# First modulation weights by rows from SP, first unit by GpSimd, rows and constants from ACT; modulated input split by token tiles

## Chip, cores and metric

One core of a Trainium2 chip runs the kernel. The metric is the device time of one execution in microseconds. The profile is of one execution on that core.

## The reference

One layer of a streaming encoder step for 256 prompt tokens and 64 sample tokens, D = 1024, all in float32. The part around the change is its opening:

```
mod = silu(c) @ w_ada + b_ada        # per sequence, w_ada is 1024 x 6144
sh1, sc1, g1, sh2, sc2, g2 = split(mod, 6)
h = rmsnorm(x, norm1_g) * (1 + sc1) + sh1
proj = h @ w_in                      # 1024 x 8192: A q|k|v, B q|k|v, two gates
```

After it come differential attention on A (8 heads, with 256 cached keys), stick-breaking attention on B (16 heads), `x += g1 * (mix @ w_out)`, a second modulated norm with `sh2, sc2`, and a hierarchical mixture of 32 experts, of which each token uses two. The rows of keys and values are outputs too.

## The kernel before

Five engines have a written program each, with semaphores between them. Tokens are padded to 384, three tiles of 128. `x_sb` holds them as rows; `xnT`, `hT_hi` and `hT_lo` hold them as columns (8 blocks k of 128 features by 384 tokens). Each float32 projection is done with three products of parts (`mm3`, L556 to L558): high by high, high by low, low by high. ACT makes a high part by a copy into the rounded type, VectorE the low part by subtracting it. For weights this is `split` (L1051 on ACT, L1339 on VectorE): it takes a unit from `raw[j]` to `w_hi[j]`, `w_lo[j]`. A unit is 384 columns of `w_in`, 128 each of q, k and v of a head, 1.5 MB, loaded by `load_unit` (L357) in three transfers whose pieces are 512 bytes. Unit h uses buffer h % 2, and unit h + 2 is loaded once `split_done` says that unit h has been split.

The opening, before attention, runs like this.

*SP* (L347 to L382) issues constants and small vectors (L347 to L352), two of the eight modulation tiles `ada_buf` (L361), x (L371, L372), nine small loads of which eight are broadcasts to 128 partitions (L374 to L377), waits for GpSimd's fills (`setup_done`), loads the router's weights (L379 to L382), then two more tiles, unit 0, four more tiles (each when its buffer has been used) and unit 1. A tile `ada_buf` is all 1024 rows by 256 columns of `w_ada`, 1 MB in pieces of 1 KB. The first eight tiles are the columns of `sh1` and `sc1`. Behind them SP waits for the transposes of x (`n_T`) and loads the caches and unit 2.

*ACT* and *VectorE* make silu(c) (L1014, L1275 to L1279), TensorE turns it and the vectors to columns (L567), and VectorE pads them (`c_cols`). Then `first_chunks` on TensorE multiplies `c_cols` (128 x 32, of which two columns are used) by four tiles at a time into four groups of 32 partitions of PSUM bank 7, in two turns of 32 matmuls of 256 columns (L561). ACT copies the result to `first_rows` (L1041), after each turn; four transposes (L605) bring it to columns; VectorE adds the bias (`mod_columns`, L1321) and makes `gain1` (L1324).

Meanwhile ACT squares x with a sum (`norm_rows`, L1024), VectorE scales the rows (`scale_rows`, L1299), TensorE transposes them (L580), and ACT and VectorE copy them to `xnT` (L1031, L1304).

The input is then modulated in place: VectorE takes k = 0 to 4 (L1309, two instructions for each k, one for each sequence) and ACT k = 5 to 7 (L1060). ACT makes `hT_hi` in four pieces of two k by 384 tokens (L1064), and VectorE `hT_lo` in the same four pieces (L1353). TensorE's first projection tile (`proj_tile`, L556) waits for each of these pieces (`h_ready`); tiles 1 and 2 need no wait then. From there `a_iteration` runs the heads of A as a pipeline on all engines.

Orders that matter: on ACT, `split(0)` stands between `norm_out` and the second copy to `first_rows`; on VectorE, `split(0, 0)` stands ahead of `mod_columns`. GpSimd has nothing from its fills (L1680 to L1688) until the first head's `rope` (L1696). The first attention buffers share memory with `xn`, and the modulation tiles share it with `hT_hi` and what follows it.

Of the kernel before, what the change touches and what calls it, by code (L numbers as in the profile page):

```python
# [7 lines left out]
P = 128  # L8
D = 1024
KD = D // P  # L10
SEQ, DEC, PAST = 256, 64, 256
TOK = SEQ + DEC
TILES = 3
# [9 lines left out]
EPS = 1e-6  # L23
NEG = -1e30
# [46 lines left out]
DVE_K = 5  # L71
# [8 lines left out]
def build(nc, t_in, t_out):  # L80
    g = t_in
    ctx = ExitStack()
    with ctx:
# [89 lines left out]
        ada_buf = [place(f"ada_buf{n}", [P, KD, ADA_COLS], F32, hT_at + 4 * KD * ADA_COLS * n) for n in range(4)]  # L173
        assert hT_at + 16 * KD * ADA_COLS <= raw_at
        first_rows = place("first_rows", [P, 2, ADA_COLS], F32, hT_at + 16 * KD * ADA_COLS)
        assert hT_at + 16 * KD * ADA_COLS + 8 * ADA_COLS <= raw_at
# [5 lines left out]
        xn = place("xn", [P, TILES, D], F32, attn_at)  # L182

# [90 lines left out]
        c_act = sem("c_act"); c_dve = sem("c_dve"); vecT_done = sem("vecT_done"); vec_ready = sem("vec_ready")  # L274
        raw_loaded = [sem(f"raw_loaded{j}") for j in range(2)]
        ada_in = [sem(f"ada_in{n}") for n in range(4)]; late_in = [sem(f"late_in{n}") for n in range(2)]
        ada_used = sem("ada_used"); late_used = sem("late_used")
        first_out = sem("first_out"); late_out = sem("late_out"); mod_T = sem("mod_T"); mod_ready = sem("mod_ready")
# [3 lines left out]
        h_full = sem("h_full"); h_hi = sem("h_hi"); h_ready = sem("h_ready")  # L282
# [31 lines left out]
        r_log = sem("r_log"); r_sub = sem("r_sub"); r_exp = sem("r_exp"); r_e2 = sem("r_e2"); r_e2x = sem("r_e2x")  # L314
        r_M = sem("r_M"); r_rank = sem("r_rank"); r_count = sem("r_count"); r_rows = sem("r_rows"); r_slot = sem("r_slot"); rounds_ready = sem("rounds_ready")
# [30 lines left out]
        def _(sp):  # L346
            sp.dma_start(cst[:], g["shape_constants"][:, 0:C_ALL]).then_inc(small_in, 16)  # L347
            sp.dma_start(vec_rows[64:72, :], g["c_prompt"].rearrange("a (k p) -> (a k) p", p=P)).then_inc(small_in, 16)
            sp.dma_start(vec_rows[72:80, :], g["c_sample"].rearrange("a (k p) -> (a k) p", p=P)).then_inc(small_in, 16)
            sp.dma_start(vec_rows[0:48, :], g["b_ada"].rearrange("(k p) -> k p", p=P)).then_inc(small_in, 16)  # L350
            sp.dma_start(vec_rows[48:56, :], g["norm1_g"].rearrange("(k p) -> k p", p=P)).then_inc(small_in, 16)
            sp.dma_start(vec_rows[56:64, :], g["norm2_g"].rearrange("(k p) -> k p", p=P)).then_inc(small_in, 16)  # L352

# [6 lines left out]
            def load_ada(c):  # L360
                sp.dma_start(ada_buf[c % 4][:], w_ada3[:, :, c * ADA_COLS:(c + 1) * ADA_COLS]).then_inc(ada_in[c % 4], 16)  # L361
# [6 lines left out]

            load_ada(0)
            load_ada(1)  # L370
            sp.dma_start(x_sb[:, 0:2, :], g["x_prompt"][0].rearrange("(t p) d -> p t d", p=P)).then_inc(x_in, 16)  # L371
            sp.dma_start(x_sb[0:DEC, 2, :], g["x_sample"][0]).then_inc(x_in, 16)  # L372
            for n, name in enumerate(("a_lam_q1", "a_lam_k1", "a_lam_q2", "a_lam_k2")):
                sp.dma_start(lam_rows[:, n, :], g[name].partition_broadcast(P)).then_inc(rows_in, 16)  # L374
            for n in range(4):
                sp.dma_start(gqk[:, n, :], g["a_qnorm_g" if n < 2 else "a_knorm_g"].partition_broadcast(P)).then_inc(rows_in, 16)
            sp.dma_start(subln[:], g["a_subln_g"].rearrange("(p a) -> p a", a=1)).then_inc(rows_in, 16)  # L377
# [1476 lines left out]
```

## Time and profile before

| | us |
|---|---|
| Median of three runs | 897.12 (896.08 to 897.85) |
| The profiled execution | 899.36 |
| Its span | 897.6 |
| TensorE busy | 739.8 (82%), 5329 matmuls |
| VectorE busy | 379.0 (42%) |
| ACT busy | 256.0 (29%) |
| GpSimd busy | 98.9 (11%) |
| Moved by transfers | 199.17 MB, mean 222 GB/s |

In the profile, PE is TensorE's matmuls and PEld its weight loads, DVE is VectorE, ACT is ScalarE, POOL is GpSimd and SP the engine that only issues transfers; SPq and POOLq are the issuing of transfers and of register work. L followed by a number is a line of the kernel. A row of the timeline gives start, duration, the instruction with output and inputs, shapes as partitions x elements, how many were merged, and in brackets how long the engine had been idle and what released it. The busy time of matmuls contains their overlap. The granted clock is a share of TensorE's full clock; its two levels are 1.2 and 2.4 GHz.

### The profile page before, as it was taken

The page shows a single profiled execution, that of the slowest core. Times are in us where ns is not written, and L with a number is a line of the kernel's source. Part 1 is how long each engine was busy: PE and PEld are TensorE (multiplying, and loading weights), DVE is VectorE, ACT ScalarE, POOL GpSimd, SP SyncE. Part 2 cuts the span into 40 slices and gives each one's busy share as a digit, 9 for nine tenths or more (in the row PEclk, how much of TensorE's full clock was granted, in tenths as well). Part 3 has the DMA queues.
Part 4 walks back from the last instruction along what each step waited for, and adds up shares of the span by engine and source line. Part 5 has one row for each costly group of instructions (what it writes and reads, how often), then busy time and mean ns, then how long its engine had stood idle before and what let it go on. Part 6 is the DMA issues. An engine that isn't in the chain of part 4 may idle for free.

```text
span 897.6 us, 13728 instructions
## 1 busy us (share of the span) xinstructions
PE 739.8 (82%) x5329; PEld 611.2 (68%) x5329; DVE 379.0 (42%) x554; ACT 256.0 (29%) x453; POOL 98.9 (11%) x156
## 2 busy tenths in 40 slices
PE   2679899999769989999998996955899878888770
PEld 1359888888659979998987996933555455464440
DVE  2243555555547553443334675561332322313223
ACT  2243444444432324543452232220111111101100
POOL 0001111111100000011100000011011010110014
PEclk9679999999999999999998998965999999999985
DMA  7955355555453649434223444089899999999805
GB/s 222 332 158 153 98 177 178 183 169 172 150 187 107 192 117 289 131 96 111 73 74 108 141 140 141 2 348 416 359 392 418 418 418 417 418 418 418 342 19 175
DMA packets 141032, 199.17 MB, mean 222 GB/s; under 512 B 11688, under 2 KB 124728, under 8 KB 128696
## 3 DMA queue, kind: packets, MB, share of 16 engines
q1 hardware_dynamic: 135208, 189.07, 60.1%
q0 software_dynamic: 5776, 9.45, 3.2%
q8 instruction: 32, 0.52, 0.2%
q14 instruction: 16, 0.13, 0.0%
HBM read 193.47 MB, written 16.55 MB: 234 GB/s over the span
## 4 chain that ended last, share of the span: by engine, by line
PE 55%; issue 23%; DVE 6%; ACT 6%; DVEq 5%; POOLq 2%; POOL 2%; ACTq 1%; DMA 0%
PE ps L561 31%; PE ps L556 6%; PE ps L557 6%; PE ps L558 6%; DVEq L1439 2%; ACT w_hi L1051 2%; DVEq L1435 1%; ACT probs L1124 1%; PE ps L936 1%; PE ps L940 1%; PE ps L972 1%; PE ps L714 1%; DVEq L1506 1%; PE ps L685 1%; DVE ss L1374 0%
## 5 line engine op out<-in xcount | busy, mean ns | idle before, releaser
L561 PE MATMUL ps<-e_w,xgT 128*64 128x256 f32 x1024 | 130.0, 418 | 32.2 <-issue 30.9
L561 PEld LDWEIGHTS ps<-e_w,xgT 128*64 128x64 f32 x1024 | 91.0, 151 | 66.9 <-issue 38.7
L1339 DVE TENSOR_TENSOR w_lo<-raw,w_hi 128x2048 fp32r<-128x2048 f32 (+1 forms) x36 | 100.1, 2780 | 35.2 <-ACT w_hi L1051 35.2
L556 PE MATMUL ps<-hT_hi,w_hi 128*128 128x320 f32 x320 | 102.2, 319 | 7.5 <-DVE w_lo L1339 7.3
L558 PE MATMUL ps<-hT_hi,w_lo 128*128 128x320 f32 x320 | 99.5, 311 | 0.0
L557 PE MATMUL ps<-hT_lo,w_hi 128*128 128x320 f32 x320 | 99.5, 311 | 0.0
L1051 ACT ACTIVATE w_hi<-raw 128x2048 fp32r<-128x2048 f32 (+1 forms) x36 | 83.4, 2316 | 54.8 <-PE ps L558 54.6
L1628 DVE TENSOR_SCALAR h_s<-h_e 128x256 f32<-128x256 f32 x16 | 4.7, 295 | 162.7 <-ACT h_e L1244 162.7
L556 PE MATMUL ps<-w_hi,hT_hi 128*128 128x384 f32 x192 | 68.2, 355 | 5.2 <-DVE hT_lo L1353 5.2
L556 PEld LDWEIGHTS ps<-hT_hi,w_hi 128*128 128x128 f32 x320 | 60.8, 190 | 9.9 <-DVE w_lo L1339 6.5
L558 PE MATMUL ps<-w_hi,hT_lo 128*128 128x384 f32 x192 | 66.1, 344 | 0.0
L557 PE MATMUL ps<-w_lo,hT_hi 128*128 128x384 f32 x192 | 66.1, 344 | 0.0
L557 PEld LDWEIGHTS ps<-hT_lo,w_hi 128*128 128x128 f32 x320 | 60.8, 190 | 0.0
L558 PEld LDWEIGHTS ps<-hT_hi,w_lo 128*128 128x128 f32 x320 | 60.7, 190 | 0.0
L561 PE MATMUL ps<-e_w,hidT 128*64 128x512 f32 x256 | 58.4, 598 | 0.6 <-ACT hidT L1250 0.6
L1244 ACT ACTIVATE h_e<-ps 128x256 f32<-128x256 f32 x16 | 6.1, 384 | 153.7 <-PE ps L561 153.7
L556 PEld LDWEIGHTS ps<-w_hi,hT_hi 128*128 128x128 f32 x192 | 37.4, 195 | 10.0 <-issue 10.0
L556 PE MATMUL ps<-oT_hi,w_hi 128*128 128x320 f32 x128 | 40.4, 316 | 1.1 <-DVE oT_lo L1465 1.1
L557 PE MATMUL ps<-oT_lo,w_hi 128*128 128x320 f32 x128 | 40.2, 314 | 0.0
L558 PE MATMUL ps<-oT_hi,w_lo 128*128 128x320 f32 x128 | 40.0, 313 | 0.0
L1793 POOL DMA_INDIRECT expert_rows<-y_sb,idx x16 | 16.3, 1017 | 215.4 <-DVE y_sb L1641 215.4
L561 PE MATMUL ps<-ada_buf,c_cols 128*32 128x256 f32 x128 | 22.8, 533 | 18.8 <-DMA ada_buf<-in_w_ada 18.8
(251 smaller groups left out, 1249.0 us busy)
## 6 DMA issues: line engine op xcount, KB each, us to landing
e_w<-in_w SPq DMA_DIRECT2D x96, 1024.0 KB, 19.6
raw<-in_w_in SPq DMA_DIRECT2D x48, 512.0 KB
ada_late<-in_w_ada SPq DMA_DIRECT2D x16, 1024.0 KB, 5.3
ada_buf<-in_w_ada SPq DMA_DIRECT2D x8, 1024.0 KB, 7.8
raw<-in_w_in SPq DMA_DIRECT2D x8, 1024.0 KB
raw<-in_w_oa SPq DMA_DIRECT2D x4, 1024.0 KB
raw<-in_w_ob SPq DMA_DIRECT2D x4, 1024.0 KB
raw<-in_w_out SPq DMA_DIRECT2D x4, 1024.0 KB
```

Source lines behind the costliest of these rows:

```text
L556: nc.tensor.matmul(out, lhs_hi, rhs_hi, start=first, stop=False, skip_group_check=True)
L557: nc.tensor.matmul(out, lhs_hi, rhs_lo, start=False, stop=False, skip_group_check=True)
L558: return nc.tensor.matmul(out, lhs_lo, rhs_hi, start=False, stop=last, skip_group_check=True)
L561: return nc.tensor.matmul(out, lhs, rhs, start=first, stop=last, skip_group_check=True)
L685: last = nc.tensor.transpose(ps[:, 4, t * P:(t + 1) * P], o_n[:, t, :], ident)
L714: last = nc.tensor.transpose(ps[:, b, c * P:(c + 1) * P], amap[:, n * P:(n + 1) * P], ident)
L936: last = nc.tensor.transpose(ps[:, 0, k * P:(k + 1) * P], xg[p % RING][:, k:D:KD], ident)
L940: last = nc.tensor.transpose(ps[:, 1, (k - 4) * P:(k - 3) * P], xg[p % RING][:, k:D:KD], ident)
L1051: A(w_hi[j][:, :, 0:width], raw[j][:, :, 0:width], ACT.Copy).then_inc(split_hi, 1)
L1339: V.tensor_tensor(w_lo[j][:, :, 0:width], raw[j][:, :, 0:width], f32(w_hi[j][:, :, 0:width]), ALU.subtract).then_inc(split_done, 1)
L1439: dve.drain()
L1793: G.indirect_dma_start(y_dram, bass.IndirectOffsetOnAxis(ap=idx[:, 1, p:p + 1], axis=0), y_sb[j][:], None, bounds_check=2 * TOK, oob_is_er ...
```

## The change

- `ada_buf` is gone. SP issues the two vectors c and then eight row blocks `ada_first[k]`: 128 rows of `w_ada` by the 2048 columns of `sh1` and `sc1`, 1 MB each in pieces of 8 KB. Three of them lie at the end of memory. TensorE's `first_columns` uses one block at a time: for each k four matmuls of 512 columns, one into each group of 32 partitions of bank 7. It waits for k = 0, 1, 2 together, for 3, 4, 5 together, for 6 and for 7. The first three k come ahead of the transposes of x, the others behind them.
- SP then issues unit 1, waits for the fills, and loads the router's weights. Before the caches it also waits for the last use of the row blocks (`ada_used`).
- ACT issues x, the constants, `b_ada` and the norm vectors at its start, and the nine small loads behind the exponential of c and ahead of the norm.
- GpSimd issues unit 0 behind its fills, with a semaphore of its own.
- ACT copies the modulation rows once (512 columns), behind `split(0)`. `lam_exp` and the sums for lambda stand behind `norm_out`.
- The modulated input goes to a buffer of its own, `h_full`, all of it by VectorE, tile by tile of tokens and in halves of four k. ACT makes `hT_hi` and VectorE `hT_lo` in the same six halves, with the multiply-adds of the next tile between the low parts. Each of the three first projection tiles waits for its two halves.
- Several semaphores are put together (`vecT_done` and `mod_T` to `col_T`; those of the router to `r_log`, `r_arg`, `r_exp`) with counts in place of names.

```diff
+ADA_GROUP = (0, 0, 0, 1, 1, 1, 2, 3)
-DVE_K = 5
...
+        ada_at = [hT_at + 8 * D * k for k in range(5)] + [(end - 24 * D) // 32 * 32 + 8 * D * k for k in range(3)]
+        ada_first = [place(f"ada_first{k}", [P, 2 * D], F32, ada_at[k]) for k in range(KD)]
+        h_full = place("h_full", [P, KD, PADDED], F32, attn_at + 4 * (2 * TILES * UNIT + 8 * P))
...
         def _(sp):
-            sp.dma_start(cst[:], g["shape_constants"][:, 0:C_ALL]).then_inc(small_in, 16)
...
+            def load_first(k):
+                sp.dma_start(ada_first[k][:], w_ada3[:, k, 0:2 * D]).then_inc(ada_in[ADA_GROUP[k]], 16)
...
-            load_ada(0)
-            load_ada(1)
...
+            for k in range(KD):
+                load_first(k)
+            load_unit(0, 1, 1)
             sp.wait_ge(setup_done, 1)
...
-            load_ada(2)
-            load_ada(3)
-            load_unit(0, 0, 0)
-            for c in range(4, 8):
-                sp.wait_ge(ada_used, c - 3)
-                load_ada(c)
-            load_unit(0, 1, 1)
...
             sp.wait_ge(n_T, KD)
+            sp.wait_ge(ada_used, KD)
...
+            def first_columns(ks):
+                for k in ks:
+                    pe.wait_ge(ada_in[ADA_GROUP[k]], 16 * ADA_GROUP.count(ADA_GROUP[k]))
+                    for j in range(4):
+                        last = mm(ps[32 * j:32 * j + 32, 7, :], c_cols[:, k, :], ada_first[k][:, j * 512:(j + 1) * 512],
+                                  k == 0, k == KD - 1)
+                    last.then_inc(ada_used, 1)
+
+            first_columns(range(3))
             pe.wait_ge(n_scaled, 3)
             for k in range(KD - 1):
                 rows_to_columns(xn, k, k).then_inc(n_T, 1)
             pe.wait_ge(n_out_a, 1)
             rows_to_columns(xn, KD - 1, 0).then_inc(n_T, 1)
-            pe.wait_ge(first_out, 1)
-            first_chunks(1)
-            pe.wait_ge(first_out, 2)
+            first_columns(range(3, KD))
+            pe.wait_ge(n_out_a, 5)
             pe.wait_ge(n_out_v, 3)
...
-                    if first and t == 0 and k % 2 == 0:
-                        pe.wait_ge(h_ready, k // 2 + 1)
+                    if first and k % 4 == 0:
+                        pe.wait_ge(h_ready, 2 * t + k // 4 + 1)
...
             A = nc.scalar.activation
+            act.dma_start(x_sb[:, 0:2, :], g["x_prompt"][0].rearrange("(t p) d -> p t d", p=P)).then_inc(x_in, 16)
+            act.dma_start(x_sb[0:DEC, 2, :], g["x_sample"][0]).then_inc(x_in, 16)
+            act.dma_start(cst[:], g["shape_constants"][:, 0:C_ALL]).then_inc(small_in, 16)
...
             act.wait_ge(small_in, 96)
             A(c_sig[64:80, :], vec_rows[64:80, :], ACT.Exp, scale=-1.0).then_inc(c_act, 1)
...
+            for n, name in enumerate(("a_lam_q1", "a_lam_k1", "a_lam_q2", "a_lam_k2")):
+                act.dma_start(lam_rows[:, n, :], g[name].partition_broadcast(P)).then_inc(rows_in, 16)
...
             act.wait_ge(x_in, 32)
             norm_rows(xn)
+            norm_out()
             act.wait_ge(lam_dve, 1)
...
+            split(0, None, None)
+            act.wait_ge(ada_used, KD)
+            A(first_rows[:], ps[:, 7, :], ACT.Copy).then_inc(n_out_a, 1)
...
+            for t in range(TILES):
+                for half in range(2):
+                    ks = slice(4 * half, 4 * half + 4)
+                    act.wait_ge(h_mod, 2 * t + half + 1)
+                    A(hT_hi[:, ks, t * P:(t + 1) * P], h_full[:, ks, t * P:(t + 1) * P], ACT.Copy).then_inc(h_hi, 1)
...
+            first_full(0, 0)
+            first_full(0, 1)
+            for t in range(TILES):
+                first_low(t, 0)
+                if t < 2:
+                    first_full(t + 1, 0)
+                first_low(t, 1)
+                if t < 2:
+                    first_full(t + 1, 1)
...
+            for n in range(3):
+                pool.dma_start(raw[0][:, :, n * P:(n + 1) * P], w_in3[:, :, n * D:n * D + P]).then_inc(unit0_in, 16)
```

`first_full(t, half)` is four multiply-adds of 128 columns into `h_full`, `first_low(t, half)` one subtraction of 512 columns behind ACT's high part of that half.

## Rows read from the trace of the kernel before

**Rows 1.** The page: the span in 40 equal slices, TensorE's busy tenths.
```profile
PE   2679899999769989999998996955899878888770
```

**Rows 2.** The list of waits, 0 to 70 us: total, times, longest.
```profile
PE ps L561 <- DMA ada_buf<-in_w_ada: 18.8, 4, 9.8
```

**Rows 3.** Windows; columns: us, engines busy (count), granted clock, DMA share, GB/s.
```profile
2.00:4.00 2.00, 0.00 (x0) 0.00 (x0) 0.00 (x0) 0.10 (x1) 0.91 (x2) 1.00 0.47 138
...
8.00:10.00 2.00, 0.00 (x0) 0.00 (x0) 0.00 (x0) 0.00 (x0) 0.00 (x0) 1.00 1.09 353
...
12.00:12.50 0.50, 0.50 (x6) 0.27 (x4) 0.00 (x0) 0.00 (x0) 0.00 (x0) 1.00 1.07 426
...
14.00:16.00 2.00, 2.00 (x14) 1.09 (x12) 0.00 (x0) 0.57 (x1) 0.00 (x0) 1.00 0.67 112
...
46.00:48.00 2.00, 2.00 (x14) 1.18 (x12) 0.00 (x0) 0.00 (x0) 0.00 (x0) 0.57 1.15 289
...
56.00:58.00 2.00, 0.62 (x2) 0.65 (x3) 1.72 (x2) 2.00 (x4) 0.00 (x0) 0.63 0.16 43
...
600.00:610.00 10.00, 5.53 (x22) 4.99 (x22) 6.58 (x32) 0.20 (x1) 0.98 (x2) 0.50 1.01 427
```

**Rows 4.** The timeline, 0 to 70 us; columns: start us, us, engine, line, operation, [idle before].
```profile
11.45 5.66 PE L561 MATMUL ps<-ada_buf,c_cols 128*32 128x256 f32 x32 [4.68 <-DMA ada_buf<-in_w_ada]
...
15.43 1.06 ACT L1024 ACTIVATE xn<-x_sb 128x1024 f32<-128x1024 f32 x1 [10.74 <-DMA x_sb<-in_x_sample]
...
19.39 2.07 DVE L1299 TENSOR_SCALAR xn<-x_sb,rstd 128x1024 f32<-128x1024 f32 x3
...
33.31 2.84 PE L580 MATMUL ps<-cst,xn 128*128 128x128 f32 x24
...
36.24 2.76 ACT L1051 ACTIVATE w_hi<-raw 128x3072 fp32r<-128x3072 f32 x1
...
39.03 3.36 DVE L1339 TENSOR_TENSOR w_lo<-raw,w_hi 128x3072 fp32r<-128x3072 f32 x1 [2.29 <-ACT w_hi L1051]
...
45.70 5.33 PE L561 MATMUL ps<-ada_buf,c_cols 128*32 128x256 f32 x32 [2.02 <-DMA ada_buf<-in_w_ada]
...
51.08 0.38 ACT L1041 ACTIVATE first_rows<-ps 128x256 f32<-128x256 f32 x1 [12.07 <-PE ps L561]
...
51.51 0.66 PE L605 MATMUL ps<-cst,first_rows 128*128 128x128 f32 x4 [0.47 <-ACT first_rows L1041]
...
52.20 0.26 DVE L1321 TENSOR_TENSOR mod<-ps,vec_cols 128x16 f32<-128x16 f32 x2 [9.81 <-PE ps L605]
...
52.89 2.83 DVE L1309 TENSOR_SCALAR xnT<-xnT,gain,mod 128x256 f32<-128x256 f32 x10 [0.17 <-issue]
...
55.40 3.05 ACT L1064 ACTIVATE hT_hi<-xnT 128x768 fp32r<-128x768 f32 x4
...
56.28 3.56 DVE L1353 TENSOR_TENSOR hT_lo<-xnT,hT_hi 128x768 fp32r<-128x768 f32 x4 [0.56 <-ACT hT_hi L1064]
...
57.38 0.66 PE L556 MATMUL ps<-w_hi,hT_hi 128*128 128x384 f32 x1 [5.21 <-DVE hT_lo L1353]
...
63.28 0.37 PE L556 MATMUL ps<-w_hi,hT_hi 128*128 128x384 f32 x1
```

**Rows 5.** The same timeline, SP's issues.
```profile
4.14 1.22 SPq L371 DMA_DIRECT2D x_sb<-in_x_prompt  x1
...
6.04 0.58 SPq L374 DMA_DIRECT2D lam_rows<-in_a_lam_q  x1
...
10.62 0.72 SPq L377 DMA_DIRECT2D subln<-in_a_subln_g  x1
```

**Rows 6.** The transfers, issues by line: count, KB each, median us to landing.
```profile
h_rows<-h2tok POOLq DMA_DIRECT2D x3, 512.0 KB, 8.5
```

**Rows 7.** The timeline, GpSimd's issues of plain transfers near the end.
```profile
873.89 0.60 POOL L1817 DMA_DIRECT2D ya<-expert_rows  x1 [2.20 <-DMA expert_rows<-y_sb,idx]
...
876.09 0.56 POOL L1817 DMA_DIRECT2D ya<-expert_rows  x1
```

More of the change, by code:

```diff
@@ L737, in _ @@
                 last = nc.tensor.transpose(ps[:, 5 + n // 4, (n % 4) * P:(n % 4 + 1) * P], late_rows[:, n * P:(n + 1) * P], ident)
-            last.then_inc(mod_T, 1)
+            last.then_inc(col_T, 1)
             pe.wait_ge(a_olo, 8)
@@ L906, in _ @@
             mm(ps[:, 0, EXPERTS:3 * EXPERTS], ones[:], flat[:, 0:2 * EXPERTS], False)
-            mm(ps[:, 0, 2 * EXPERTS:3 * EXPERTS], ones[:], M[:, 0, :], False).then_inc(r_rank, 1)
+            mm(ps[:, 0, 2 * EXPERTS:3 * EXPERTS], ones[:], M[:, 0, :], False).then_inc(r_log, 1)
             for t in range(TILES):
                 last = mm(ps[:, 1, 0:EXPERTS], ones[:], M[:, t, :], t == 0, t == 2)
-            last.then_inc(r_count, 1)
+            last.then_inc(r_log, 1)
             def slot_table(r):
@@ L1329, in _ @@
             scale_rows(xn, 1)
+            norm_out()
+            dve.wait_ge(rows_in, 144)
+            for n in range(2):
+                V.tensor_tensor(lam_prod[:, n, :], lam_rows[:, 2 * n, :], lam_rows[:, 2 * n + 1, :], ALU.mult)
+            V.tensor_scalar(gqk[:, 0:2, :], gqk[:, 0:2, :], 0.125, None, ALU.mult)
+            V.tensor_scalar(subln[:], subln[:], 1.0 - LAM_INIT, None, ALU.mult)
+            dve.drain()
+            V.tensor_reduce(lam_sum[:], lam_prod[:], AX, ALU.add).then_inc(lam_dve, 1)
             dve.wait_ge(lam_act, 1)
@@ L1342, in _ @@
             split(0, 0)
[L1343 to L1344 removed]
+            dve.wait_ge(col_T, 2)
+            mod_columns(0, [ps[:, 5, :].rearrange("p (m j s) -> p j m s", m=4, j=4)[:, :, :, 0:2]],
                         gain1, 8, 48)
@@ L1347, in _, with first_full, first_low @@
             dve.wait_ge(n_out_v, 4)
-            for k in range(DVE_K):
-                modulate(xnT, xnT[:, k, :], k, gain1, 0).then_inc(h_full, 1)
-            for n in range(4):
-                ks = slice(2 * n, 2 * n + 2)
-                dve.wait_ge(h_hi, n + 1)
-                V.tensor_tensor(hT_lo[:, ks, :], xnT[:, ks, :], f32(hT_hi[:, ks, :]), ALU.subtract).then_inc(h_ready, 1)
+            def first_full(t, half):
+                for k in range(4 * half, 4 * half + 4):
+                    last = V.tensor_scalar(h_full[:, k, t * P:(t + 1) * P], xnT[:, k, t * P:(t + 1) * P], gain1[:, k, t // 2:t // 2 + 1],
+                                           mod[:, k, t // 2:t // 2 + 1], ALU.mult, ALU.add)
+                last.then_inc(h_mod, 1)
+            def first_low(t, half):
+                ks, sl = slice(4 * half, 4 * half + 4), slice(t * P, (t + 1) * P)
+                dve.wait_ge(h_hi, 2 * t + half + 1)
+                V.tensor_tensor(hT_lo[:, ks, sl], h_full[:, ks, sl], f32(hT_hi[:, ks, sl]), ALU.subtract).then_inc(h_ready, 1)
+            first_full(0, 0)
[7 more added lines that the diff above has]
+                    first_full(t + 1, 1)
             def combine(parts, f):
@@ L1568, in _ @@
             tt(eh2[:], etie[:], bc(etm[:], 8), ALU.is_equal)
-            V.tensor_tensor(e2[:], m2[:], m1[:], ALU.subtract).then_inc(r_e2, 1)
+            V.tensor_tensor(e2[:], m2[:], m1[:], ALU.subtract).then_inc(r_arg, 1)
             for n, eh in enumerate((eh1, eh2)):
```

104 lines of the change are left out of this document (32 added, 72 removed).

## The prediction

> **What bounds the kernel now.** I read the page first. In its forty slices TensorE is at seven tenths or more nearly everywhere, except for two holes: the first two slices (0 to 45 us) and two slices at 583 to 628 us, the router and the first experts [rows 1]. The change works in the first hole. There the list of waits for 0 to 70 us says what TensorE lacks: 18.8 us in four waits for tiles of the modulation weights, by far its longest [rows 2]. The windows say why. The transfers run at their limit, but the rate depends on what is moved: 353 GB/s with the 1 KB pieces of the modulation tiles, 426 with the 4 KB rows of x, 289 with the 512 B pieces of a projection unit, and 427 near 600 us with expert weights; at 14 to 16 us it falls to 112 GB/s behind small transfers [rows 3]. So the opening is bound by transfers and by what stands ahead of what in SP's queue. Last I read the timeline from the last modulation matmul (starts at 45.70, ends at 51.03) to the first projection matmul at 57.38; from there TensorE works without a hole of note, with the granted clock at 0.5, and returns to its full level at 63.28 [rows 4]. Whatever makes 57.38 earlier should move the whole rest: nothing behind it waits for a time of its own, only for earlier work.
>
> The profiled execution took 899.36 us with a span of 897.6; the median is 897.12. I work out a shift of the span and subtract it from the median. Some 0.2% (1.8 us) can be told from no change.
>
> **Part 1, transfers ahead of the last modulation row.** Before, the eight 1 MB column tiles share SP's queue with x, nine small loads (eight of them broadcasts), four router loads and unit 0's three. After, SP issues two tiny loads and then eight row blocks (one k each, 8 KB pieces); x, constants and broadcasts go by ACT, unit 0 by GpSimd, and unit 1 and the router stand behind. Large pieces ahead of the end are 8.39 MB of weights, 1.31 of x and 0.25 of constants, 9.95 MB. Bounds are 28.2 us at 353 GB/s and 23.4 at 426; 8 KB pieces are nearest to the 4 KB rows of x, so I take 415 GB/s: 24.0 us. Unit 0 is 1.57 MB; if it shares the engines in that time it adds 5.4 us at 289 GB/s, if it comes wholly behind, nothing; I take 5.4. The broadcasts add at most the 1.3 us of the row at 14 to 16 us (0.67 of two microseconds) and at least nothing; I take 1.3 with a little for the b_ada and norm rows, 1.5. The stream starts within the window from 2 to 4 us, where 138 GB/s ran [rows 3]: 2.5. From the last byte to the semaphore I allow 1.5 (no row has it alone; ends 0 and 2). Sum: the last row block lands at 2.5 + 24.0 + 5.4 + 1.5 + 1.5 = 34.9 us. Call it T.
>
> The Trainium skill (DMA: Bandwidth & Descriptors, Specifications) puts the limit of HBM per core at about 358 GB/s. By that the large pieces would take 27.8 us and the gain would be 3.8 us smaller. The rows at 426 and 427 GB/s do not agree with it, so the sum does not use it.
>
> **Part 2, from T to the first projection matmul.** Thirty-two matmuls of 256 columns took 5.66 us at 11.45, or 0.177 each; of 512 columns 0.354. The fourth group's four matmuls take 1.4 us. Earlier row blocks arrive every 3 us and need 1.4 each, so TensorE has kept up by T: k 3 to 5 wait for one another, but the 16 matmuls of k 3 to 6 are 5.7 us and the two blocks behind them take about 6 to arrive. Then, by the timeline [rows 4]: ACT copies 512 columns in one piece (0.38 us for 256, so 0.6), four transposes 0.66 and 0.1 between them: T + 2.8. Modulation columns and gain took from 52.20 to ahead of 52.89, about 0.6 with their drains, the same here: T + 3.4. Before, VectorE then did ten multiply-adds in 2.83 us (ACT six beside it), ACT the high parts in 3.05 us for four of 768 columns, VectorE the low parts in 3.56. After, four multiply-adds of 128 columns (0.28 mean before for longer ones, so 0.2 each) end at T + 4.2, ACT's first high part (512 columns, 0.55) at T + 4.8, VectorE's second four at T + 5.0, its first low part (0.6) at T + 5.7, and TensorE starts at T + 5.8 = 40.7. The old stretch from the last matmul was 57.38 - 51.03 = 6.35 us, the new one 4.4: splitting by token tiles is worth 2.0, the queues the rest. Gain: 57.38 - 40.7 = **16.7 us**.
>
> All multiply-adds now go to VectorE, 24 of 0.2 us and six low parts of 0.6, so 1.4 us per half of a tile. TensorE needs 3.8 us for that half at the slow clock (12 matmuls, 0.32 apart) and 2.1 at the full one. The six halves hide behind it; if that cover were gone they would cost 5 to 6 us.
>
> **Part 3, the clock.** Before, TensorE paused 5.2 us ahead of the projection, the clock fell in the window 56 to 58 (0.63 there, 0.50 after), and 57.38 to 63.28 ran at the 1.2 GHz level: at 2.4 GHz that is 2.95 us less. Now the pause is 3.0 us. It may keep the clock (gain 2.95) or not (0). I take **1.5**.
>
> **Part 4, what is moved and must stay hidden.** *ACT* issues x, its sample, constants and three small loads: x took SP 1.22 us and a small one 0.58, so some 4.1 us for the six [rows 5], while nothing is there to compute. Then nine small issues stand between the sigmoid's exponential and the norm; on SP they went from 6.04 to 11.34, 5.3 us. Behind them the norm takes 4.0 (from 15.43 to the scaling at 19.39), scaling 2.1, 24 transposes 2.8 [rows 4]. If constants land at 10.5 (1.6 MB at half of 400 GB/s from 2.5 on), the norm starts at 16, scaling ends at 22 and transposes at 25; cost 0 behind the weights that arrive until 34.9. *Unit 0*: ACT's split of 2.76 us stands ahead of the copy of modulation rows, and VectorE's of 3.36 ahead of the modulation columns [rows 4]. They cost 0 if unit 0 has landed 6.2 us ahead of T + 2.8, by 31.5 us. Its waits queue both engines' whole rest, so each later microsecond costs one. A transfer issued by GpSimd beside a busy queue is shown by the stores of 512 KB: 8.5 us to landing [rows 6], 62 GB/s; by that, unit 0 lands at 3.2 (GpSimd's last two fills lie in the window 2 to 4) + 25.4 + 2 = 30.6, just in time, and with an even share near 15. Bounds 0 and the price in the rival below; I take 0. *SP* now waits for the last use of the row blocks before the caches and unit 2: 36.3 plus unit 1's 5.4 us, while ACT needs unit 1 at about 46 and unit 2 at about 59 (17 us ahead of the old times): 0. The router is wanted near 590. The semaphores put together late in the kernel keep their order: 0.
>
> **Sum:** 16.7 + 1.5 = 18.2 us; 897.1 - 18.2 = 878.9, forecast **879.0**.
>
> **Rivals.** *Unit 0 comes late.* For it: the three loads are 3072 pieces of 512 B against 64 large ones per transfer engine, and the 62 GB/s above. If its share is half of that (31 GB/s), 0.85 MB is there when the weights end at about 31, the other 0.72 MB goes beside unit 1 at 145 GB/s, and it lands at 37.5. Then 6.2 for the splits and 2.9 for modulation and the first half: TensorE starts at 46.6, the gain is 10.8, the time 886.3. Against it: its issue starts as early as the weights'. The Trainium skill (DMA: Bandwidth & Descriptors, Queues, rings and completion order) has each transfer engine go round its queues a packet at a time; if SP's packets are the larger ones, that would give GpSimd such a small share. No row of this trace shows packets of that kind.
>
> *Constants or x come late.* They have one queue, constants behind x, and the sigmoid waits for all. From their landing s the ACT path needs 0.3 + 5.3 + 4.0 + 2.1 + 2.8 = 14.5, then 20 matmuls of 7.1 us: s + 21.6 against T + 1.4 = 36.3. So from s = 14.7 each microsecond costs one. Three even shares give 1.6 MB at 137 GB/s, s = 14.2, on the edge. At s = 20 the cost is 5.3 and the time 884.2. For it: x took until 15.43 before; against: it was issued 4 us later then and stood behind 2 MB.
>
> *Slower: GpSimd makes the pieces too slowly.* GpSimd took 0.60 us for an issue with 128 pieces and 0.56 for one with 64 [rows 7]. If all of 0.60 were per piece (4.7 ns), unit 0 would need 14.4 us; the two rows speak for far less. Break-even is a landing at 57.4 - 9.1 = 48.3, which is 14 ns a piece; at 20 ns it lands at 66, TensorE starts at 75.5, and the time is 915.
>
> *It does nothing*: the transfers' total sets the end whatever their order. For it speaks that the engines were saturated; against, that 1.57 MB of unit 1 and the router are now behind, and the wasted windows gone.
>
> **Chances.** Forecast (876 to 882) 0.52; unit 0 late 0.20; constants late 0.20; nothing 0.03; slower 0.05. Range: fast end with 426 GB/s, no broadcasts and the full clock, 18.2 + 0.6 + 1.5 + 1.4 = 21.7, and 3 more if unit 0 takes less of the engines: 872.5. Slow end: both late cases, 888.5. Faster 0.92, same 0.03, slower 0.05.
>
> **What would show it.** First projection matmul near 41 (right between 37 and 44); last row block's matmuls from about 35; ACT's first split before 31.5; the stretch between them 4.4 us; ACT's norm at about 16; a rate near 415 GB/s until 30 us. TensorE waiting for low parts inside the first unit would refute part 2; an unchanged distance from that first matmul to the end is the premise, and if it grows by over 2 us the premise is wrong.

## The result: 8.2 us faster, where 18.1 were forecast

The changed kernel took 888.42 us (median of 4 runs, 888.03 to 889.46), the kernel before in the same session 896.60 (4 runs, 896.04 to 897.85): ratio 0.9907, 95% interval 0.9892 to 0.9921. The sign was right. The time lies on the upper edge of the range (872.5 to 888.5), 9.4 us from the forecast of 879.0, and the gain is less than half of the forecast one. The profiled execution took 888.03 us with a span of 886.3; before it was 899.36 and 897.6.

TensorE's slices on the page of the changed kernel answer to [rows 1]:

```profile
PE   0589999998789889999998978864899788798770
```

The first slice (22 us) holds next to no matmul, the second half, and the third is at eight tenths. The hole at 600 us is as it was. The waits of the opening (engine, what it waited for: us in total, times, longest), against [rows 2]:

```profile
ACT c_sig L1000 <- DMA vec_rows<-in_norm_g: 11.5, 1, 11.5
ACT lam_exp L1029 <- DVE lam_sum L1315: 7.1, 1, 7.1
DVE lam_prod L1311 <- DMA subln<-in_a_subln_g: 5.7, 1, 5.7
PE ps L585 <- ACT first_rows L1043: 4.8, 1, 4.8
PE ps L545 <- DMA ada_first<-in_w_ada: 2.5, 2, 1.3
```

TensorE's wait for modulation weights fell from 18.8 us to 2.5. In its place stands a wait that no part of the prediction has: VectorE's first lambda operation waits 5.7 us for the last of the nine small loads, ACT's lambda exponential waits 7.1 us for VectorE, and TensorE waits 4.8 us for ACT's copy of the modulation rows. The kernel before had the first of these waits too, where it held nothing up: unit 0 was split only at 36.24 [rows 4].

```profile
18.55 0.36 DVE L1290 TENSOR_TENSOR lam_prod<-lam_rows 128x64 f32<-128x64 f32 x2 [10.98 <-DMA subln<-in_a_subln_g]
```

The timeline of the opening (start, duration, engine, line, operation, tiles, count, idle time before and its releaser), to be laid beside [rows 4]:

```profile
16.95 0.30 ACT L1000 ACTIVATE c_sig<-vec_rows 16x128 f32<-16x128 f32 x1 [11.48 <-DMA vec_rows<-in_norm_g]
...
20.66 5.24 PE L545 MATMUL ps<-ada_first,c_cols 128*32 128x512 f32 x24 [1.33 <-DMA ada_first<-in_w_ada]
20.72 0.45 ACTq L1023 DMA_DIRECT2D subln<-in_a_subln_g  x1
21.28 1.06 ACT L1010 ACTIVATE xn<-x_sb 128x1024 f32<-128x1024 f32 x1 [4.02 <-issue]
...
27.31 2.84 PE L564 MATMUL ps<-cst,xn 128*128 128x128 f32 x24 [1.41 <-DVE xn L1277]
...
34.92 1.07 PE L545 MATMUL ps<-ada_first,c_cols 128*32 128x512 f32 x8 [1.20 <-DMA ada_first<-in_w_ada]
...
36.46 0.36 DVE L1311 TENSOR_TENSOR lam_prod<-lam_rows 128x64 f32<-128x64 f32 x2 [5.72 <-DMA subln<-in_a_subln_g]
...
37.42 0.20 ACT L1029 ACTIVATE lam_exp<-lam_sum 128x2 f32<-128x2 f32 x1 [7.06 <-DVE lam_sum L1315]
37.53 2.75 ACT L1039 ACTIVATE w_hi<-raw 128x3072 fp32r<-128x3072 f32 x1
...
40.18 0.58 ACT L1043 ACTIVATE first_rows<-ps 128x512 f32<-128x512 f32 x1
40.30 3.36 DVE L1324 TENSOR_TENSOR w_lo<-raw,w_hi 128x3072 fp32r<-128x3072 f32 x1 [2.26 <-ACT w_hi L1039]
...
43.58 0.18 DVE L1299 TENSOR_TENSOR mod<-ps,vec_cols 128x32 f32<-128x32 f32 x1
...
44.19 2.14 DVE L1337 TENSOR_SCALAR h_full<-xnT,gain,mod 128x128 f32<-128x128 f32 x8 [0.17 <-issue]
...
47.08 0.66 PE L540 MATMUL ps<-w_hi,hT_hi 128*128 128x384 f32 x1 [5.15 <-DVE hT_lo L1345]
```

Read it from the middle. The last row block has landed at 34.92, where T was forecast as 34.9, and its matmuls end at 35.99. From there the forecast goes 4.4 us to the first projection matmul; the trace takes 11.1. ACT stood idle from 30.35 until 37.42. In its program the order is: copies of the transposed x, lambda exponential, split of unit 0, copy of the modulation rows. In VectorE's it is: lambda block, low part of unit 0, modulation columns. Both programs put the first wait for the nine small loads ahead of unit 0's split, so the 2.75 and 3.36 us that should have been hidden ran after the weights had landed. From 43.58 on the order is that of the forecast again, in 3.50 us where the forecast has 3.0.

The transfers (how each was issued, count, KB of one, median us to landing), the packets on GpSimd's queue from 0 to 45 us (count, MB, share), and two-microsecond stretches of the windows (busy time of the engines, granted clock, DMA share, GB/s):

```profile
raw<-in_w_in POOLq DMA_DIRECT2D x3, 512.0 KB, 14.4
...
lam_rows<-in_a_lam_q ACTq DMA_DIRECT2D x2, 32.0 KB, 10.1
...
gqk<-in_a_qnorm_g ACTq DMA_DIRECT2D x2, 32.0 KB, 15.9
```

```profile
q0 software_dynamic: 432, 1.57, 9.2%
```

```profile
14.00:16.00 2.00, 0.00 (x0) 0.00 (x0) 0.00 (x0) 0.00 (x0) 0.00 (x0) 1.00 1.05 368
...
22.00:24.00 2.00, 2.00 (x12) 0.45 (x8) 0.00 (x0) 2.00 (x5) 0.00 (x0) 1.00 1.04 403
...
50.00:52.00 2.00, 2.00 (x7) 2.00 (x7) 2.00 (x8) 0.88 (x2) 0.00 (x0) 0.50 0.47 117
```

The stretch at 14 us with 112 GB/s [rows 3] is gone. The eight broadcasts of 32 KB, issued by ACT beside SP's row blocks, took 7.9 to 16.0 us to land (the rows give medians of two). Unit 0, the load that the prediction feared for, was issued in three transfers from 3.73 on, and the last of them landed at 23.6, long before ACT could split it. The prediction counted 3072 pieces of 512 bytes for it; on GpSimd's queue stand 432 packets for its 1.57 MB.

### The profile page after: what moved, and what is told of

It is laid out like the page before. It is cut to its first block, busy times and chain, and to the rows that moved or that the text cites. A ratio compares the mean times of both kernels' runs of the same rounds, so it can differ in the third digit from the quotient of the medians.

```text
span 886.3 us, 13607 instructions
## 1 busy us (share of the span) xinstructions
PE 727.3 (82%) x5265; PEld 601.5 (68%) x5265; DVE 382.6 (43%) x569; ACT 254.1 (29%) x448; POOL 101.2 (11%) x159
## 4 chain that ended last, share of the span: by engine, by line
PE 54%; issue 22%; ACT 6%; DVE 5%; DVEq 5%; POOL 2%; POOLq 2%; DMA 2%; SPq 1%; ACTq 1%
PE ps L545 31%; PE ps L540 6%; PE ps L542 6%; PE ps L541 6%; DVEq L1441 2%; ACT w_hi L1039 2%; DVEq L1437 1%; PE ps L916 1%; SPq L353 1%; ACT probs L1110 1%; PE ps L920 1%; DMA raw<-in_w_in 1%; PE ps L952 1%; DVEq L1508 1%; DMA out_a_v_sample<-stage 1%
## 5 line engine op out<-in xcount | busy, mean ns | idle before, releaser
L540 PEld LDWEIGHTS ps<-w_hi,hT_hi 128*128 128x128 f32 x192 | 37.0, 193 | 10.1 <-issue 10.1
L545 PEld LDWEIGHTS ps<-e_w,hidT 128*64 128x64 f32 x256 | 17.5, 136 | 29.6 <-issue 27.8
```

Source lines behind the costliest of these rows:

```text
L540: nc.tensor.matmul(out, lhs_hi, rhs_hi, start=first, stop=False, skip_group_check=True)
L545: return nc.tensor.matmul(out, lhs, rhs, start=first, stop=last, skip_group_check=True)
```

## The experiments

**Theory A:** the lambda wait, that is the landing of the nine small loads on a queue beside large pieces, holds unit 0's split, and costs some 7 us. **Rival B:** the late constants (16.95 instead of 10.5) are the cause, since they delay everything on ACT. **Rival C:** unit 0 by GpSimd takes the engines' time, or the token split brings nothing.

**Lambda late (e1).** The lambda block goes behind the six halves on VectorE, and its exponential behind the high parts on ACT; nothing else changes.

```diff
 # shortened; ACT
-            act.wait_ge(lam_dve, 1)
-            A(lam_exp[:], lam_sum[:], ACT.Exp).then_inc(lam_act, 1)
 def split ... split(0) ... first_rows ... high parts
+            act.wait_ge(lam_dve, 1)
+            A(lam_exp[:], lam_sum[:], ACT.Exp).then_inc(lam_act, 1)
 # DVE: the block from wait_ge(rows_in, 144) to neg_lam likewise,
 # from ahead of split(0, 0) to behind the loop of first_low and first_full
```

> The changed kernel took 888.4 us, with the first projection matmul at 47.08, although the last weight row block landed as forecast (its matmuls end at 35.99). Here the wait for the nine small loads, the sums for lambda and the exponential move behind the six halves of the modulated input on VectorE and ACT. Theory A (the lambda wait, met at 36.46 by the landing of the last small load, holds ACT's split of unit 0 from about 30.5 to 37.53): ACT's split starts at 30 to 31, the first projection matmul at 41 to 42, time 882 to 883. Rival B (constants landing at 16.9 delay the ACT path and with it everything): nothing moves, 888. Rival C (unit 0 from GpSimd lands only at about 36 to 37): the split still starts at 36 to 37, 887 to 888.

It took 881.11 us (879.3 to 881.14, 5 runs); ratio 0.9841 [0.982, 0.986], against 895.66 of the kernel before. Its timeline:

```profile
16.24 0.30 ACT L1000 ACTIVATE c_sig<-vec_rows 16x128 f32<-16x128 f32 x1 [10.92 <-DMA vec_rows<-in_norm_g]
...
29.54 2.76 ACT L1037 ACTIVATE w_hi<-raw 128x3072 fp32r<-128x3072 f32 x1
...
34.03 1.06 PE L545 MATMUL ps<-ada_first,c_cols 128*32 128x512 f32 x8 [1.02 <-DMA ada_first<-in_w_ada]
...
36.51 0.19 DVE L1300 TENSOR_TENSOR mod<-ps,vec_cols 128x32 f32<-128x32 f32 x1 [0.83 <-PE ps L585]
...
40.01 0.66 PE L540 MATMUL ps<-w_hi,hT_hi 128*128 128x384 f32 x1 [3.54 <-DVE hT_lo L1335]
```

The split runs at 29.54, under the weights, and the first projection matmul starts 7.1 us earlier than in the changed kernel. Of that, 0.9 us is not the wait: the last row block's matmuls start at 34.03 instead of 34.92. From the end of these matmuls to the first projection matmul it is 4.92 us instead of 11.09, so the wait is worth 6.2. The constants were as late as there (16.24), and it cost nothing: the split still ended ahead of the last row block. That shows A and takes away B as a cause. The interval lies clear of that of the changed kernel (0.9892 to 0.9921).

**Constants ahead of x (e2).** ACT issues constants and norm rows first, then x.

```diff
+            act.dma_start(cst ...); act.dma_start(vec_rows ...)   # three of them
             act.dma_start(x_sb[:, 0:2, :], ...)
             act.dma_start(x_sb[0:DEC, 2, :], ...)
-            act.dma_start(cst ...); act.dma_start(vec_rows ...)   # three of them
```

> ACT issues the constants, b_ada and the norm vectors ahead of x, nothing else is changed. Theory A: constants land by 7, the exponential of c and with it the nine small issues come about 10 us sooner (from 7 instead of 17), the last of them lands before 31, so the lambda wait is met in time: first projection matmul at 41 to 42, 882 to 883. Rival B expects the same time, but with the gain from the c path. Rival C: 888. If the small loads are starved by SP's large pieces until these end near 35, whenever they are issued, the wait is met at 35 to 36 and the time stays at 887 to 888.

888.85 us (888.18 to 894.38, 7 runs), ratio 0.994 [0.9919, 0.9962]: no better than the changed kernel.

```profile
7.51 0.30 ACT L1000 ACTIVATE c_sig<-vec_rows 16x128 f32<-16x128 f32 x1 [2.27 <-DMA vec_rows<-in_norm_g]
...
10.40 5.47 ACTq L1022 DMA_DIRECT2D gqk<-in_a_knorm_g  x2
15.90 5.27 ACTq L1023 DMA_DIRECT2D subln<-in_a_subln_g  x1
...
24.53 1.06 ACT L1010 ACTIVATE xn<-x_sb 128x1024 f32<-128x1024 f32 x1 [16.71 <-DMA x_sb<-in_x_sample]
...
39.17 0.36 DVE L1311 TENSOR_TENSOR lam_prod<-lam_rows 128x64 f32<-128x64 f32 x2 [3.73 <-DMA subln<-in_a_subln_g]
```

The constants landed 9.4 us earlier, and the first small load was issued 9.4 us earlier; yet lambda started 2.7 us later. x, issued at 2.65 instead of 0.82 and so behind the first row block's issue, came only at 24.5, and the small loads stood behind it on ACT's queue: the first of them landed at 28.1. ACT's last two kinds of issue took 5.47 and 5.27 us, where they take 0.94 and 0.45 in the changed kernel, so the issue of the last one, for which lambda waits, ended at 21.17 in both. This run therefore tells little of an earlier issue. It shows that constants ahead of x bring nothing; theory A's 882 did not come, and the time lies near the 887 to 888 that stood for small loads starved by large pieces.

**Token split alone (e3).** The kernel before with only the split by token tiles (its queues as they were).

```diff
 # shortened
-            for k in range(DVE_K): modulate(...)      # whole rows of 384 tokens, ACT the rest
+            first_full(0, 0); first_full(0, 1); for t in range(TILES): first_low ... first_full
-                    if first and t == 0 and k % 2 == 0: pe.wait_ge(h_ready, k // 2 + 1)
+                    if first and k % 4 == 0: pe.wait_ge(h_ready, 2 * t + k // 4 + 1)
```

> The kernel before with one part of the change alone: modulated input in a buffer of its own, by VectorE, in six halves of token tiles. The changed kernel shows 3.5 us from the modulation columns to the first projection matmul, before it was 5.2. Theory (part 2 of the prediction): worth 1.7 to 2.0 us, 894.7 against 896.6. Rival: VectorE's larger share makes TensorE wait inside the first unit, or the clock falls sooner, and nothing is gained, 896.6.

893.53 us (889.9 to 899.81, 12 runs), ratio 0.9983 [0.9967, 1.0]. The stretch from the modulation columns to the first projection matmul:

```profile
52.68 0.26 DVE L1319 TENSOR_TENSOR mod<-ps,vec_cols 128x16 f32<-128x16 f32 x2 [10.07 <-PE ps L606]
...
56.25 0.48 PE L557 MATMUL ps<-w_hi,hT_hi 128*128 128x384 f32 x1 [3.61 <-DVE hT_lo L1357]
```

It is 3.57 us, where before it was 5.18 (52.20 to 57.38, [rows 4]): 1.6 us, and the median agrees with about that, though its interval just reaches 1.

**The other way round (e7).** e1 with the modulation of the kernel before, and TensorE's waits for its four pieces.

```diff
 # shortened
-            first_full(0, 0); first_full(0, 1); for t in range(TILES): first_low ... first_full
+            for k in range(DVE_K): modulate(...)      # whole rows of 384 tokens, ACT the rest
```

> The version with the lambda part late, with the modulated input as in the kernel before (in place, five k on VectorE, three on ACT, pieces of two k by 384 tokens). On the kernel before, the token tiles gave 2.1 us (893.5 against 895.7, interval ending at no change). Theory: without them the first projection matmul is 1.7 us later, 882.8 against 881.1, and the change of the queues alone, once its wait is out of the way, is worth the other 13. Rival: the six halves bring nothing here, 881.1.

884.3 us (881.87 to 889.59, 5 runs), ratio 0.9858 [0.9832, 0.9884].

```profile
37.51 0.19 DVE L1305 TENSOR_TENSOR mod<-ps,vec_cols 128x32 f32<-128x32 f32 x1 [1.28 <-PE ps L587]
...
42.62 0.66 PE L542 MATMUL ps<-w_hi,hT_hi 128*128 128x384 f32 x1 [5.15 <-DVE hT_lo L1334]
```

From the columns to the projection 5.11 us against 3.50 in e1: 1.6 us again. The last row block's matmuls start 1.0 us later than in e1 (35.03), with the same transfers. The two medians differ by 3.2 us, on two chips, and their intervals overlap, so the split's worth is read from the stretch.

**Unit 0 by SP behind the row blocks (e4).**

```diff
-            for n in range(3): pool.dma_start(raw[0] ...)   # ahead, on GpSimd
+            for n in range(3): sp.dma_start(raw[0] ...)     # on SP, ahead of unit 1
```

> The changed kernel with unit 0 issued by SP, behind the eight row blocks and ahead of unit 1, in place of GpSimd. Theory A: the last row block lands 4 to 5 us sooner (about 31), unit 0 only some 6 us behind it, near 37, so the split starts at about 37 by another wait, and the first projection matmul stays near 46 to 47: 887 to 889. Rival C (GpSimd's transfer was the late one): sooner by 2 us or more, under 886.5.

886.24 us (883.98 to 891.0, 6 runs), ratio 0.9899 [0.988, 0.9919].

```profile
36.33 2.76 ACT L1041 ACTIVATE w_hi<-raw 128x3072 fp32r<-128x3072 f32 x1 [3.26 <-DMA raw<-in_w_in]
...
45.89 0.66 PE L542 MATMUL ps<-w_hi,hT_hi 128*128 128x384 f32 x1 [5.15 <-DVE hT_lo L1347]
```

Without unit 0 beside them the last row block landed at 28.9 instead of 34.9; the prediction's price for sharing was 5.4 us. TensorE used it up at 31.2 without waiting for it, held by the transposes. But then unit 0 itself is the last to land and the split starts at 36.33, 1.2 us earlier than in the changed kernel. GpSimd's loads cost T about what was priced and are not the cause. The median lies just under the 886.5 that stood for rival C, but its interval overlaps that of the changed kernel, and the trace has unit 0 later than there, not sooner.

**The nine small loads by SP ahead of the row blocks (e5).**

```diff
+            for n, name in enumerate(("a_lam_q1", ...)): sp.dma_start(lam_rows ...)   # and gqk, subln
             for k in range(KD): load_first(k)
-            for n, name in enumerate(("a_lam_q1", ...)): act.dma_start(lam_rows ...)  # and gqk, subln
```

> The changed kernel, lambda wait in its place, but the nine small loads issued by SP ahead of the row blocks, not by ACT behind the exponential of c. With the constants first on ACT they had been issued from 7.5 and still landed only at 39.2. Theory (on ACT's queue they land only when SP's large pieces end; on SP's queue, ahead of them, they do not wait): the last lands before 20, the lambda wait costs nothing, the split of unit 0 starts at 26 to 30, and the first projection matmul is at 41 to 44, since the row blocks are issued some 5 us later while x and unit 0 use the engines: 881.5 to 885. Rival (it is the place of the wait alone and small loads are slow on any queue): 888.

886.48 us (885.16 to 892.42, 6 runs), ratio 0.9901 [0.9872, 0.993].

```profile
6.00:8.00 2.00, 0.00 (x0) 0.00 (x0) 0.00 (x0) 0.00 (x0) 0.59 (x1) 1.00 0.66 174
8.00:10.00 2.00, 0.00 (x0) 0.00 (x0) 0.00 (x0) 0.00 (x0) 0.00 (x0) 1.00 0.61 188
...
38.00:40.00 2.00, 1.98 (x20) 0.68 (x24) 1.42 (x8) 0.79 (x2) 0.00 (x0) 1.00 0.27 99
```

```profile
38.27 0.35 DVE L1311 TENSOR_TENSOR lam_prod<-lam_rows 128x64 f32<-128x64 f32 x2
...
49.05 0.66 PE L545 MATMUL ps<-w_hi,hT_hi 128*128 128x384 f32 x1 [3.54 <-DVE hT_lo L1345]
```

Lambda no longer waits for a transfer, as A says. But the last row block's matmuls start at 43.06 instead of 34.92, and the first projection matmul comes 2.0 us later. The trace shows three things on the way. SP issues its first row block at 7.61 instead of 1.64, behind the nine. The rate from 6 to 10 us is 174 and 188 GB/s, where the changed kernel has 253 and 379. And the last row block comes in apart: a transfer lands in sixteen parts, and of this one twelve had landed by 37.1 and the last at 43.0 (34.1 to 34.9 in the changed kernel), while the engines were busy for 0.27 of the time from 38 to 40 us. What held these few engines is open. The wait went, and its price came back through the transfers.

**Row blocks in pieces of 2 KB (e8).** If small pieces wait their turn behind 8 KB pieces of another queue, shorter pieces there must bring the small loads in sooner, with the same bytes and the same issuing engines.

```diff
-                sp.dma_start(ada_first[k][:], w_ada3[:, k, 0:2 * D]) ...
+                for q in range(4):
+                    sp.dma_start(ada_first[k][:, q * 512:(q + 1) * 512], ...)
...
-                    pe.wait_ge(ada_in[ADA_GROUP[k]], 16 * ADA_GROUP.count(ADA_GROUP[k]))
+                    pe.wait_ge(ada_in[ADA_GROUP[k]], 64 * ADA_GROUP.count(ADA_GROUP[k]))
```

> The changed kernel with each row block loaded by four transfers of 512 columns, so SP's pieces are 2 KB, not 8 KB; order, bytes and the lambda wait stay. Theory (the pieces of ACT's queue take turns with SP's, so a small load pays for a large piece each time: the eight broadcasts are 64 pieces for each of 16 transfer engines and took from about 17 to 35.5, 0.29 us each, and an 8 KB piece at 410 GB/s over 16 engines takes 0.32): with 2 KB pieces the constants land by 12 instead of 17 and the last small load by 26 instead of 36.4, the split of unit 0 starts when the norm's copies are out, at 24 to 28, and the first projection matmul is at 40 to 43, 881 to 884. Rival (small loads are slow whatever stands beside them, or ACT's queue is served last): the lambda wait ends at 34 to 37 again, 887 to 889.

887.06 us (884.0 to 890.37, 6 runs), ratio 0.9897 [0.9874, 0.9919]. Its issues and its timeline:

```profile
lam_rows<-in_a_lam_q ACTq DMA_DIRECT2D x2, 32.0 KB, 7.7
...
gqk<-in_a_qnorm_g ACTq DMA_DIRECT2D x2, 32.0 KB, 9.2
```

```profile
11.17 0.31 ACT L1001 ACTIVATE c_sig<-vec_rows 16x128 f32<-16x128 f32 x1 [5.77 <-DMA vec_rows<-in_norm_g]
...
33.03 0.35 DVE L1312 TENSOR_TENSOR lam_prod<-lam_rows 128x64 f32<-128x64 f32 x2
...
39.88 1.07 PE L546 MATMUL ps<-ada_first,c_cols 128*32 128x512 f32 x8 [1.66 <-DMA ada_first<-in_w_ada]
```

The broadcasts landed in 7.7 to 10.0 us instead of 10.1 to 15.9 (medians of two), the constants let the sigmoid start at 11.17 instead of 16.95, and lambda waited for no transfer. The last small load landed at 27.3 instead of 36.4; 5.8 us of that is its earlier issue, 3.3 its faster landing. The spacing tells more. In the changed kernel the first four broadcasts landed 2.6 us apart (24.9, 27.5, 30.2, 32.8), and 0.3 to 0.4 us apart once the last row block had landed at 34.9; with 2 KB pieces all eight landed 0.8 to 1.1 us apart. So the size of the pieces beside them sets their pace. The gain is given back: the rate at 10 to 16 us is 312 to 324 GB/s where the 8 KB pieces had 347 to 371, and the last row block comes 5.0 us later. The median is that of the rival (887 to 889), and the forecast of 881 to 884 failed by the row blocks. The Trainium skill (DMA: Bandwidth & Descriptors, Queues, rings and completion order) says that a transfer engine serves its queues in turn, a packet at a time; e8 agrees in kind, and no run here shows how large a packet is.

**A warm clock (e6, e10).** e1 and four matmuls of 512 columns between the transposes and the projection, into a bank that is free.

```diff
             last.then_inc(col_T, 1)
+            for _ in range(4):
+                mm(ps[:, 6, :], ident, first_rows[:, 0:512], True)
```

> The version with the lambda part late (881.1 us, first projection matmul at 40.01), with four matmuls of 128x128 by 512 columns on finished data into an idle bank, between the transposes of the modulation rows and the first projection tile (their result is not used). Part 3 of the prediction: TensorE's pause of 3.5 us there let the granted clock fall to 0.5 until 45.5, with matmuls 0.32 us apart for 0.175. If the pause is the cause, the clock stays at its full level, that stretch is 2.5 to 2.9 us shorter, and the time is 878.3 to 878.8. Rival: the level depends on the thinner work ahead of the pause (waits for row blocks), the clock falls anyway, 881, or 882 if the four get in the way.

e6 took 880.02 us (878.27 to 885.83, 5 runs), ratio 0.9816 [0.9793, 0.9839]. Against e1's 0.9841 that decided nothing, so both were run again, on one chip with the changed kernel.

> The changed kernel once more, unchanged, on the same chip as the three below, so that they can be compared with it: 888.4 us, first projection matmul at 47.

> The version with the lambda part late, unchanged, beside the changed kernel on one chip: 7 us less than it (881.3 against 888.4), as the places of the first projection matmul say (40.0 against 47.1).

> The version with the lambda part late and four filling matmuls, unchanged, beside the version without them. With the filling, the clock stayed at its full level from the transposes on, and the first tile's matmuls ran 0.175 us apart. Theory: 1.5 to 2.7 us less than the version without (878.6 to 880). Rival (the 1.1 us between the two medians came from the chips): the same time.

The kernel before took 896.58 us there (11 runs), and e8 above belongs to the same series. The changed kernel: 885.87 (884.15 to 890.52, 6 runs), 0.9889 [0.9865, 0.9913]. e9, which is e1: 880.55 (879.61 to 884.06, 5 runs), 0.9837 [0.9812, 0.9863]. e10, which is e6: 880.33 (879.24 to 880.92, 5 runs), 0.9825 [0.9804, 0.9846]. The changed kernel showed the same wait again:

```profile
37.00 0.36 DVE L1311 TENSOR_TENSOR lam_prod<-lam_rows 128x64 f32<-128x64 f32 x2 [6.24 <-DMA subln<-in_a_subln_g]
```

The window from 42 to 44 us and GpSimd's multiplication by the norm gains (minimum, median and maximum ns; first and last start) in e9:

```profile
42.00:44.00 2.00, 2.00 (x8) 2.00 (x7) 2.00 (x7) 0.94 (x2) 0.00 (x0) 0.50 0.73 213
```

```profile
L1700 POOL TENSOR_TENSOR stage<-stage,gqk x8: 1839/1850/1853, 60.2 to 215.2; 128x768 f32<-128x768 f32 x8
```

and in e10:

```profile
42.00:44.00 2.00, 2.00 (x13) 2.00 (x13) 2.00 (x8) 0.70 (x2) 0.00 (x0) 1.00 0.63 176
```

```profile
L1702 POOL TENSOR_TENSOR stage<-stage,gqk x8: 1844/1849/1860, 57.4 to 212.3; 128x768 f32<-128x768 f32 x8
```

(There the last row block's matmuls end at 36.69 and the first projection matmul starts at 47.61; in e9 these are 35.43 and 40.76.) The filler kept the clock at its full level, and the work that follows the first unit came 2.8 us earlier and stayed so until 215 us; 0.2 of that is the start of the projection (40.52 against 40.76). At the first matmul of the output projection nothing of it was left (250.60 in e9, 250.38 in e10). The stretch between took 35.4 us in e9 and 38.1 in e10, but also 35.0 and 38.0 in two executions of the kernel before (its trace and b1 below), so a single pair of traces can't tell whether the filler lengthened it. The medians are the same, where 1.5 to 2.7 us had been expected.

**The kernel before again (b1)**, one execution, for what differs from one to the next.

> The kernel before once more, for a second profile. Its first profile took 899.36 us, 2 to 4 us more than its timed runs. If the excess lies in the opening, the first projection matmul is near 57.4 again with a long time, or at 54 to 55 with a short one, and the distance from there to the end stays at 839 to 840. If it lies behind the opening, that distance varies by some 3 us.

898.9 us, span 897.2, first projection matmul at 58.01, and from it to the end 839.2 us (840.2 in the trace of the kernel before). It is again 2.9 us above its median (896.04). Over all fourteen traces the rest behind the first projection matmul takes 838.1 to 839.3 us in the four whose execution was within 0.6 us of its kernel's median (the changed kernel, e1, e9, e10), and 839.2 to 845.3 in the other ten, whose executions were 2.8 to 6.3 us above. So at least a part of such an excess lies behind the opening.

## Why the prediction was half right

- *What bounds the kernel:* right. The stretch from the first projection matmul to the end was 840.2 us before and 839.2 after (839.3 in e1): what the opening gives, the rest keeps. It is no constant, though: 841.2 in the changed kernel's second trace, 843.4 in e4, 845.3 in e7.
- *Part 1, transfers:* right, T = 34.9 forecast and 34.92 measured. It is partly luck: the rate was 347 to 379 GB/s from 8 to 16 us and 400 to 415 from 22 on, where 415 was taken throughout, and other terms made up for it. Its 5.4 us for unit 0 is borne out by e4, where the last row block landed 6.0 us earlier.
- *Part 2, from T to the projection:* 40.7 forecast, and e1 has it at 40.01 (e9 at 40.76). From the end of the last row block's matmuls it takes 4.92 us (5.33 in e9) where I had 4.4: mostly, the multiply-adds took 0.27 us each, not 0.2. The token split is worth 1.6 us, not 2.0. TensorE did not wait for a low part inside the first unit. In the changed kernel the step does not hold: see part 4.
- *Part 3, the clock:* 1.5 taken, 0 came. The granted clock is 0.50 in the window from 50 to 52 us. The stretch's own worth of 2.95 us is about right (2.5 in e10), but it does not reach the median.
- *Part 4, what must stay hidden:* **here the prediction failed.** The step says of the nine small loads that their issues take 5.3 us and leaves it at that; it follows ACT's chain through the norm and the transposes to 25 us and gives "cost 0 behind the weights that arrive until 34.9". It never asked when these loads land and who waits for them. The last landed at 36.4, and the wait stands ahead of unit 0's split on both engines. Measured from the end of the last row block's matmuls it cost 11.09 - 4.92 = 6.2 us (5.6 by a1 and e9); the medians say 5.3 on one chip (885.87 - 880.55) and 7.3 across two sessions. That is nearly all of the 6.4 us by which the first projection matmul missed its forecast (47.08 against 40.7). The trace before could have warned: there VectorE waited 11.0 us for the same small load, until 18.55.
- *The constants* were late, 16.95 against 10.5, and by the rival's own rule each microsecond from 14.7 on should have cost one: 2.3 us. It cost nothing (e1). By the rule the last row block's matmuls end 21.6 us behind the constants, at 38.6. In the trace the way through the transposes took 13.2 us and not 14.5, and the 20 matmuls behind them, which I had priced at 7.1 us from a row of matmuls with half the columns [rows 4], took 3.64 and 1.07 (a matmul of 512 columns stands there as two records, hence x32 and x8). That is 34.9, and TensorE still waited 1.2 us for the last row block.
- *The rivals:* unit 0 late (886.3) gives nearly the measured time, but unit 0 was there at 23.6. The right number would have had the wrong cause: what the case shares with it is only the place, the split ahead of the modulation rows. GpSimd's pieces came at no great price, and "does nothing" and "slower" fell.
- *The sum:* 18.2 less 6.2 for the wait and 1.5 for the clock is 10.5. The first projection matmul came 10.3 us earlier, the profiled pair says 11.3 and the medians 8.2. The kernel before has a profiled execution 2.8 us above its median (899.36 to 896.60), and the changed kernel's first has not (888.03 to 888.42), though its second has (890.52 to 885.87 in a1). So a shift read from a profiled pair is not the shift of the medians. The 2 us between 10.5 and 8.2 stay unexplained.

The best version is e1: 0.984 of the time of the kernel before, and against the changed kernel on one chip 5.3 us less, for moving one block of eight small operations. e10 is equal to it.

## What to carry to other kernels

When transfers are moved to other queues, price for each the time at which it lands and find the first instruction that waits for it, also for the smallest: a 32 KB load may need 16 us beside 8 KB pieces. In an engine's program put a wait for something that is needed late behind the work that is needed now; here that order alone was worth 5 to 7 us. Three attempts to bring the load in earlier were worth nothing: in two (e5, e8) the large transfers came later by nearly as much or more (5.0 and 8.1 us), and in the third (e2) the load itself came no earlier. Forecast from medians if there are some, and keep the profiled execution for shifts within a stretch.

## What the runs showed of the hardware

- The landing of small transfers depends on the piece size of another queue. Each of the eight broadcasts is 128 pieces of 256 B, 8 for each of 16 transfer engines. Beside 8 KB pieces they landed 2.6 us apart, 0.33 us a small piece; at 410 GB/s one of 16 engines needs 0.32 us for 8 KB. Beside 2 KB pieces (e8) they landed some 0.9 us apart, 0.11 us a small piece; at 315 GB/s 2 KB need 0.10. That is an estimate, and it fits one small piece for each large one. The first of them took 7.9 us to land, and 7.2 in e8, so this part does not go by the piece size.
- Issuing can itself stall: with x still on its way on ACT's queue, its issues of `gqk` and `subln` took 5.47 and 5.27 us (e2) against 0.94 and 0.45. In the changed kernel SP's three issues of unit 1, behind eight row blocks, took from 6.45 to 35.2.
- The parts of one transfer can land far apart: with the nine small loads ahead of the row blocks (e5), the last row block's sixteen parts landed from 35.7 to 43.0, in the changed kernel from 34.1 to 34.9.
- A load of 512 B runs that GpSimd issued stands in the trace as 432 packets for 1.57 MB, and its three transfers landed a median of 14.4 us after issue beside 8 KB pieces.
- TensorE paused 3.5 us ahead of the projection (e1, e9), and the projection began at a granted clock of 0.50; with four matmuls in the pause (e10) it began at 1.00. The 2.5 us that this saved were not to be found at 250 us, nor in the median.
- The twelve matmuls at 20.66 took 5.24 us (0.44 each), the sixteen at 30.08 of the same shape 3.64 (0.23 each), both at a granted clock of 1.00, and the weight loads between them took 0.23 and 0.13. In e9 the weight loads go from 0.22 to 0.14 us within the first twelve, which took 4.07. TensorE had done one matmul before the slow ones and 24 transposes just before the fast ones; no run varies that.
